# Turning the experts' middle rows with VectorE's 32x32 blocks and GpSimd moves instead of TensorE transposes

## What is computed

```
def _swiglu(x, w_gate, w_up, w_down):
    return (jax.nn.silu(x @ w_gate) * (x @ w_up)) @ w_down

def _moe(x, router, w_gate, w_up, w_down):
    xf = x.reshape(B * T, D)                       # 320 x 1024
    logits = (xf @ router).astype(jnp.float32)
    top_v, top_i = lax.top_k(logits, TOP_K)        # 2 of 8
    gates = jax.nn.softmax(top_v, axis=-1)
    combine = jnp.sum(jax.nn.one_hot(top_i, N_EXPERTS) * gates[..., None], axis=1)
    for e in range(N_EXPERTS):
        y = y + combine[:, e:e + 1] * _swiglu(xf, w_gate[e], w_up[e], w_down[e])
```

## Time and profile before

| | us |
|---|---|
| median of 3 runs | 1573.74 (1573.68 to 1573.88) |
| the profiled execution | 1574.41 |
| its span | 1572.9 |
| PE busy | 1554.9 (99%) |
| VectorE busy | 1296.5 (82%) |
| ScalarE busy | 1029.6 (65%) |
| GpSimd busy | 57.0 (4%) |
| mean granted clock of TensorE | 0.997 of full |

### The profile page before, as it was taken

The page is one execution under the profiler, slowest core; times in us unless marked ns, Lnnn a source line. Parts: engine busy times, 40 slices in busy tenths (PEclk is TensorE's granted clock), DMA queues, the critical chain, the costliest instruction groups (busy, mean ns, idle before and its releaser), DMA issues.

```text
span 1572.9 us, 23445 instructions
## 1 busy us (share of the span) xinstructions
PE 1554.9 (99%) x8467; PEld 1374.8 (87%) x8467; DVE 1296.5 (82%) x1534; ACT 1029.6 (65%) x1192; POOL 57.0 (4%) x89
## 2 busy tenths in 40 slices
PE   9999999999999999999999999999999999999997
PEld 8999999999989998888788888888888888888886
DVE  5578876766675678999899988989998999998996
ACT  4455433333354557788678878778778778777785
POOL 1002000000020010000200000000000001000000
PEclk9999999999999999999999999999999999999999
DMA  9625944444534344999999999999999999999992
GB/s 280 196 81 203 364 136 160 135 158 134 160 108 134 108 141 176 375 368 387 391 396 394 389 372 380 396 392 368 383 370 370 395 397 383 380 395 394 386 395 104
DMA packets 229906, 457.49 MB, mean 291 GB/s; under 512 B 10930, under 2 KB 73088, under 8 KB 229760
## 3 DMA queue, kind: packets, MB, share of 16 engines
q1 hardware_dynamic: 224288, 434.16, 76.3%
q0 software_dynamic: 5520, 22.04, 3.6%
HBM read 441.74 MB, written 17.58 MB: 292 GB/s over the span
## 4 chain that ended last, share of the span: by engine, by line
PE 91%; DVE 5%; DMA 2%; ACT 1%; issue 1%; SPq 0%; DVEq 0%; ACTq 0%
PE ps L1083 18%; PE ps L1058 12%; PE ps L1060 12%; PE ps L1059 12%; PE ps L681 11%; PE ps L683 10%; PE ps L682 10%; DVE wlo L1540 2%; PE ps L1096 1%; DMA raw<-in_moe_w_up 1%; DVE wlo L1535 1%; DMA proj<-in_x_prompt 0%; PE ps L1132 0%; ACT whi L1182 0%; PE ps L859 0%
## 5 line engine op out<-in xcount | busy, mean ns | idle before, releaser
L1540 DVE TENSOR_TENSOR wlo<-raw,whi 128x1024 fp32r<-128x1024 f32 x672 | 779.5, 1220 | 48.8 <-ACT whi L1186 47.5
L1186 ACT ACTIVATE whi<-raw 128x1024 fp32r<-128x1024 f32 x672 | 675.0, 1054 | 69.8 <-PE ps L1083 40.5
L1058 PE MATMUL ps<-whi,xg 128*128 128x512 f32 x896 | 354.7, 396 | 1.9 <-DVE wlo L1540 1.9
L1060 PE MATMUL ps<-whi,xg 128*128 128x512 f32 x896 | 350.1, 391 | 0.0
L1059 PE MATMUL ps<-wlo,xg 128*128 128x512 f32 x896 | 349.6, 390 | 0.0
L681 PE MATMUL ps<-xh,whi 128*128 128x322 f32 (+1 forms) x832 | 260.4, 313 | 1.6 <-DVE x L1928 1.1
L683 PE MATMUL ps<-xh,wlo 128*128 128x322 f32 (+1 forms) x832 | 257.6, 310 | 0.0
L682 PE MATMUL ps<-xl,whi 128*128 128x322 f32 (+1 forms) x832 | 257.6, 310 | 0.0
L1535 DVE TENSOR_TENSOR wlo<-raw,whi 128x2048 fp32r<-128x2048 f32 x72 | 165.0, 2293 | 55.3 <-ACT whi L1182 55.1
L1060 PEld LDWEIGHTS ps<-whi,xg 128*128 128x128 f32 x896 | 168.6, 188 | 36.0
L1058 PEld LDWEIGHTS ps<-whi,xg 128*128 128x128 f32 x896 | 168.6, 188 | 35.7 <-DVE wlo L1540 2.3
(11 more groups left out here) (368 smaller groups left out, 1470.9 us busy)
## 6 DMA issues: line engine op xcount, KB each, us to landing
raw<-in_moe_w_gate SPq DMA_DIRECT2D x112, 1024.0 KB, 8.7
raw<-in_moe_w_up SPq DMA_DIRECT2D x112, 1024.0 KB, 9.2
raw<-in_moe_w_down SPq DMA_DIRECT2D x112, 1024.0 KB, 8.7
raw<-in_w_in SPq DMA_DIRECT2D x23, 1024.0 KB, 6.1
raw<-in_ffn_w_gate SPq DMA_DIRECT2D x14, 1024.0 KB, 5.0
raw<-in_ffn_w_up SPq DMA_DIRECT2D x14, 1024.0 KB, 5.1
raw<-in_ffn_w_down SPq DMA_DIRECT2D x14, 1024.0 KB, 5.0
raw<-in_w_out SPq DMA_DIRECT2D x8, 1024.0 KB, 5.0
```

The costliest lines, as they stand in the source:

```text
L1058: pe.matmul(bank[:], xh_k, wh, start=k == 0, stop=False)
L1060: mm = pe.matmul(bank[:], xl_k, wh, start=False, stop=k == KT - 1)
L1186: act.activation(part(whi, n, SPLIT, h), part(raw, n, RAW, h), ACT.Copy).then_inc(hi_ready, 1)
L1540: dve.tensor_tensor(part(wlo, n, SPLIT, h), part(raw, n, RAW, h), part(whi, n, SPLIT, h).bitcast(F32), ALU.subtract).then_inc(lo_ready, 1)
```

## The change

In pairs 1 to 3, for chunks 1 to 12 of 14 (TURNED), TensorE no longer turns hm. Step "Z" (after down 0 of chunk c): VectorE transposes hm in 32x32 blocks within SBUF into hz, each block staying in its place of 32 partitions. GpSimd waits for it and copies 16 pieces of 32 partitions x 4 x 32 numbers to the partitions where they belong, into hT, also in SBUF. Step "R" (after gate 1 of the next chunk): ScalarE rounds hT into hT_hi, and VectorE makes hT_lo = hT - hT_hi. TensorE waits for hT_lo_ready before "down". Pair 0 keeps the old order (FIRST), and so do chunks 0 and 13 of each pair. hz and hT lie in u_mem, which earlier stages use.

On GpSimd, the copies of chunk c stand in line with the parks; the load of the next pair's rows comes after chunk 8's copies instead of right after the first park, and in the last pair GpSimd waits for its fetches to land before it goes on copying. To make room for three new semaphores, kd_turned, v_turned, kd_read and v_read are no longer kept per layer.

```diff
-    def pair_steps(last):
+    TURNED = range(1, PC - 1)
+
+    def pair_steps(first=False, last=False):
         steps = []
         for c in range(PC):
             steps.append(("gate", c, 0))
-            if c:
+            if c == 1 or c and first:
                 steps.append(("T", c - 1, 0))
             steps.append(("gate", c, 1))
+            if c > 1 and not first:
+                steps.append(("R", c - 1, 0))
...
             elif c:
-                steps += [("down", c - 1, 0), ("down", c - 1, 1)]
+                steps.append(("down", c - 1, 0))
+                if not first:
+                    steps.append(("Z", c, 0))
+                steps.append(("down", c - 1, 1))
...
+        hz = u_mem[:, 0:4 * P]
+        hT = u_mem[:, 4 * P:8 * P].rearrange("p (f s) -> p f s", f=4)
...
+            def turn_blocks(c, i):
+                pool.wait_ge(hz_ready, upto(c, i, PER_TURNS))
+                pool.wait_ge(hT_lo_ready, upto(c - 1, i, PER_TURNS))
+                pool.nop(nofuse=True)
+                z = hz.rearrange("p (f j s) -> p f j s", f=4, j=4)
+                for j in range(4):
+                    for q in range(4):
+                        ins = pool.tensor_copy(hT[32 * j:32 * j + 32, :, 32 * q:32 * q + 32], z[32 * q:32 * q + 32, :, j, :])
+                ins.then_inc(hT_copied, 1)
+
+            def pair(i):
+                for c in TURNED:
+                    turn_blocks(c, i)
+                    if c == 7:
+                        park(i, 0, y_parked)
+                    if c == 8:
+                        load_rows(i + 1 if isinstance(i, int) else pool.snap(i + 1))
                 park(i, 1, y_parked)
                 pool.wait_ge(y_parked, upto(48, i, 32))
...
             pool.wait_ge(rows_known, 1)
             fetch(0, y_1)
-            park(pairs, 0, last_parked)
-            pool.wait_ge(last_parked, 16)
-            fetch(1, y_2)
             for t in range(TT):
-                pool.wait_ge(y_fetched[1][t], 16)
+                pool.wait_ge(y_fetched[0][t], 16)
+            for c in TURNED:
+                turn_blocks(c, pairs)
+                if c == 7:
+                    park(pairs, 0, last_parked)
+                    pool.wait_ge(hT_copied, upto(c, pairs, PER_TURNS))
+                    pool.nop(nofuse=True)
+                    pool.wait_ge(last_parked, 16)
+                    fetch(1, y_2)
+                    for t in range(TT):
+                        pool.wait_ge(y_fetched[1][t], 16)
...
+                    if part == "R":          # ScalarE
+                        act.wait_ge(hT_copied, upto(c, i, PER_TURNS))
+                        act.activation(hT_hi[:, c % 2, :, :], hT, ACT.Copy).then_inc(hT_hi_ready, 1)
+                        continue
...
+                    if part == "Z":          # VectorE
+                        dve.wait_ge(m_hid, upto(c + 2, i, PC))
+                        dve.wait_ge(hT_copied, upto(c - 1, i, PER_TURNS))
+                        dve.transpose(hz, hm[:, c % 2, :]).then_inc(hz_ready, 1)
+                        continue
+                    if part == "R":
+                        turns += 1
+                        dve.wait_ge(hT_hi_ready, upto(turns, i, PC))
+                        dve.tensor_tensor(hT_lo[:, c % 2, :, :], hT, hT_hi[:, c % 2, :, :].bitcast(F32), ALU.subtract
+                                          ).then_inc(hT_lo_ready, 1)
+                        continue
...
-                            pe.wait_ge(job_read, upto(turned[c], i, PER_JOBS))
+                            if first or c not in TURNED:
+                                pe.wait_ge(job_read, upto(turned[c], i, per_jobs))
+                            else:
+                                pe.wait_ge(hT_lo_ready, upto(c, i, PER_TURNS))
```

More of the change, by code:

```diff
@@ L112, in pair_steps, with units_of, jobs_of @@
             elif c:
-                steps += [("down", c - 1, 0), ("down", c - 1, 1)]
+                steps.append(("down", c - 1, 0))
+                if not first:
+                    steps.append(("Z", c, 0))
+                steps.append(("down", c - 1, 1))
         return steps + [("down", PC - 1, 0), ("down", PC - 1, 1)]
-    PAIR, FINAL = pair_steps(False), pair_steps(True)
-    UNITS = [s for s in PAIR if s[0] in ("gate", "up", "down")]
-    assert UNITS == [s for s in FINAL if s[0] in ("gate", "up", "down")]
+    def units_of(steps):
+        return [s for s in steps if s[0] in ("gate", "up", "down")]
+    def jobs_of(steps):
+        return sum(s[0] in ("T", "X", "GT") for s in steps)
+    FIRST, PAIR, FINAL = pair_steps(first=True), pair_steps(), pair_steps(last=True)
+    UNITS = units_of(PAIR)
+    assert UNITS == units_of(FINAL) == units_of(FIRST)
     PER_PAIR = len(UNITS)
-    PER_JOBS = len(PAIR) - PER_PAIR
-    LAST_JOBS = len(FINAL) - PER_PAIR
-    assert PER_PAIR % RAW == 0 and PER_PAIR % SPLIT == 0 and PER_JOBS % 2 == 0
+    PER_JOBS = jobs_of(PAIR)
+    PER_TURNS = len(TURNED)
+    assert PER_PAIR % RAW == 0 and PER_PAIR % SPLIT == 0 and PER_JOBS % 2 == 0 and jobs_of(FIRST) % 2 == 0
     ctx = ExitStack()
@@ L339, in hybrid_stream_step @@
         proj_ready, gate_act, gate_dve = (by_layer(n) for n in ("proj_ready", "gate_act", "gate_dve"))
-        kd_turned, v_turned, kd_read, v_read, score_done, score_read = (by_layer(n) for n in (
-            "kd_turned", "v_turned", "kd_read", "v_read", "score_done", "score_read"))
+        kd_turned, v_turned, kd_read, v_read = (sem(n) for n in ("kd_turned", "v_turned", "kd_read", "v_read"))
+        score_done, score_read = (by_layer(n) for n in ("score_done", "score_read"))
         ds_done, st_step, o_done, o_sq, ms_act, og_step = (by_layer(n) for n in (
@@ L802, in turn_kv @@
                                               ident[:])
-                        mm.then_inc(v_turned[l], 1)
+                        mm.then_inc(v_turned, 1)
                 def scores():
-                    pe.wait_ge(v_read[l], 1)
+                    pe.wait_ge(v_read, 3 * l + 1)
                     for h in range(VT):
                         mm = pe.transpose(ps[6][0:DEC, P * h:P * h + P], proj[:, TV + h, 2 * P:T], ident[:])
-                    mm.then_inc(v_turned[l], 1)
-                    pe.wait_ge(kd_read[l], 2)
+                    mm.then_inc(v_turned, 1)
+                    pe.wait_ge(kd_read, 2 * l + 2)
                     for n, (t, pair) in enumerate((t, pair) for t in range(2) for pair in range(PAIRS)):
@@ L842, in states @@
                                 mm.then_inc(score_done[l], 1)
-                    pe.wait_ge(v_read[l], 3)
+                    pe.wait_ge(v_read, 3 * l + 3)
                     for t in range(LAST // 2):
@@ L1038, in pair @@
             def pair(i, steps, first=False):
-                unit, job = 0, GATHERS
+                unit, job, per_jobs = 0, *((GATHERS, jobs_of(FIRST)) if first else (FIRST_JOB, PER_JOBS))
                 for part, c, half in steps:
                     a, fc = c // FC, c % FC
+                    if part in ("Z", "R"):
+                        continue
                     if first and (part, c, half) == ("gate", 1, 0):
@@ L1163, in _ @@
             router()
-            pair(0, PAIR, first=True)
+            pair(0, FIRST, first=True)
             pe.wait_ge(ctl_ready, 1)
@@ L1692, in read_kd @@
                 def read_kd():
[L1693 to L1696, removed]
+                    dve.wait_ge(kd_turned, 2 * l + 1)
+                    dve.tensor_copy(kd_tok[:, 0:512], ps[4][:]).then_inc(kd_read, 1)
+                    dve.wait_ge(kd_turned, 2 * l + 2)
+                    dve.tensor_copy(kd_tok[0:DEC, 512:768], ps[5][0:DEC, 0:256]).then_inc(kd_read, 1)
                 def mask_scores():
@@ L2262, in _ @@
             step = router()
-            pair(0, PAIR, step, first=True)
+            pair(0, FIRST, step, first=True)
             dve.wait_ge(ctl_ready, 1)
```

37 lines of the change are left out of this document (22 added, 15 removed).

## The result

| | before | after |
|---|---|---|
| median, us | 1573.71 (4 runs) | 1719.08 (4 runs, 1718.05 to 1720.22) |
| ratio | | 1.0925, 95% interval 1.0911 to 1.0938 |
| span of the profiled execution | 1572.9 | 1718.3 |
| PE, VectorE, ScalarE, GpSimd busy | 99, 82, 65, 4% | 93, 77, 60, 24% |

The changed kernel is 145.4 us slower. The prediction was 1725, with 1590 to 1805 as range.

What follows compares the result with a forecast made beforehand. PE (TensorE), fed without a gap, was taken to bound the kernel before, VectorE's period after. Sum: 1574.4 + 144 (36 chunks) - 6 (stock) + 4 + 9 (last pair) = 1725.4, 1725 against the median; range 1590 to 1805.

Steps and rivals of the forecast that it cites:

- TensorE's saving, 0.47 us a chunk: On PE, four transposes leave each of 36 chunks, 0.47 us a chunk, 16.9 us on the path.
- Block transpose, 0.60 us: VectorE's added 128x512 transpose in step Z was taken to cost 0.60 us a chunk, like hm.
- Price of a copy, 0.30 us: One undisturbed GpSimd copy of 32 partitions x 128 elements was taken at 0.30 us, between 0.10 and 0.53.
- Copies done in the window, 4 of 16: Between Z and hT_lo, four copies get in at six boundaries of VectorE's subtractions; the other 12 run while VectorE waits.
- Toll, 0.10 us a copy: Each copy pushed in between subtractions delays VectorE's next instruction about 0.10 us, 0.4 us a chunk for four.
- The stand: VectorE stands ahead of hT_lo for 12 x 0.30 = 3.6 us of copies and 0.65 us for ScalarE's hT_hi.
- Chunk, 20.8 us: VectorE's period sets the chunk: 15.74 + 0.4 + 3.6 + 0.65 + 0.4 = 20.8 us against 16.8, 144 us over 36.
- Last pair, 4 + 9 us: Last pair: 4 us once for chunk 8's copies after the fetches, 9 us for VectorE's eight extra instructions.
- Swallowed by the stock, -6: In each of three pairs, PE's units in stock swallow the first 2 us of delay, -6 us.
- The clock costs nothing: A half clock after PE's gaps of 3 to 5 us a chunk fits into its idle time and costs nothing.
- (a): Rival: copies slip in, hT_hi is ready in time, PE stays the bound, 1559 us; chance 0.15.
- (b): Rival: all 16 copies end in the window but each holds VectorE 0.1 us, 1594 us; chance 0.10.

Runs made afterwards that it cites:

- one copy: Changed kernel with only the last of each chunk's 16 GpSimd copies left in, the other 15 blocks of hT keeping old values: 1564.97 us, ratio 0.9944 to the kernel before.
- the runs with 4, 8 and 16 copies: Changed kernel with four or eight of each chunk's 16 GpSimd copies left in: 1572.5 and 1627.7 us; 16 is the changed kernel itself, 1719.08 us.
- the run with memsets: Changed kernel with each chunk's 16 GpSimd copies replaced by 24 memsets, 16 into hT and 8 into a free part of u_mem: 1568.3 us.
- the run with TensorE kept busy: Changed kernel with 13 idle matmuls into a free bank in TensorE's gap before "down" of chunks 1 to 11: 1717.75 us, ratio 1.0912.
- every third chunk: Changed kernel turning only chunks 2, 5, 8, 11 of pairs 1 and 2 the new way, with ten subtractions in the window; other pairs as before: 1590.87 us.
- one copy and the last pair as before: Changed kernel with one of 16 copies left in for pairs 1 and 2, last pair turning and fetching as before the change: 1562.99 us, ratio 0.9932.

## Why the prediction was right

*TensorE's saving, 0.47 us a chunk.* Right: 16.32 instead of 16.80 us with one copy, 11.5 us over 24 chunks.

*Block transpose, 0.60 us.* It takes 0.63 us to the next row, and no more than 710 ns:

```profile
L2215 DVE STREAM_TRANSPOSE u_mem<-hm x36: 702/706/710, 869.1 to 1672.1; 128x512 f32<-128x512 f32 x36
```

*Price of a copy, 0.30 us.* 0.33 alone.

*Copies done in the window, 4 of 16.* Wrong for 33 of the 36 chunks: six, one at each boundary, the sixth as VectorE stops (in three of them a few more slip into a short pause of VectorE). I had read the 3.62 us row as a boundary lost, and weighed the Trainium skill's rule (SBUF — State Buffer, "Who interferes with whom": whoever comes first has the pair) down by it. The chunks of pairs 1 and 2, and the runs with 4, 8 and 16 copies there, agree with the strict queue. But boundaries are lost as well, as in the earlier trace rows: four in a row in chunks 5 and 11 of the last pair, with two copies done. What makes a waiting read miss them stays open. The same section of the Trainium skill says that a GpSimd instruction which only writes does not contend with such a VectorE instruction; the run with memsets agrees, with 0.20 us for each.

*Toll, 0.10 us a copy.* 0.08 (1.30 against 1.22 us), five times a chunk: 0.4. The predicted 0.4 was four times 0.10.

*The stand.* Predicted 12 x 0.30 = 3.6 us of copies and 0.65 for hT_hi; measured 3.5 (ten copies and the tail of the sixth) and 0.67 of the 4.17 us ahead of hT_lo. Too many copies left over (12) at too low a price (0.30) made nearly the right sum, which is luck: by the same working, six in the window and 0.33 each give 15.74 + 0.4 + 3.3 + 0.65 + 0.4 = 20.5.

*Chunk, 20.8 us.* 20.5, so 36 x 3.7 = 133 us instead of 144.

*Last pair, 4 + 9 us.* From the starts of its copies, chunk 8 came 3.4 us late and the chunks with combine and its like 10.5 us in sum: 13.9 against 13. Some 2 of the 10.5 us are not VectorE's extra work but the copies that missed boundaries in chunks 5 and 11 (VectorE's extra standing less the toll saved); they stand in for part of the predicted 9. In pair 1, ScalarE's three scalings of acc, which I had not counted, took 0.6 us each.

*Swallowed by the stock, -6.* Too much. 133.2 + 13.9 + 1.7 = 148.8 against 145.4 measured leaves -3.4. The first hm of pairs 1, 2 and 3 starts at 854.9, 1137.9 and 1418.2 us, before the change at 856.3, 1093.5 and 1330.6. So 1.4 us of the 3.4 were gained ahead of pair 1, where the first hm starts at 854.2 to 856.5 us in all these runs, and about 2 us are left for all three pairs together, where I had 2 for each.

*The sum.* 1725 against 1719 is closer than its terms: the chunk was 11 us too dear over 36 chunks, and against that the stock took 4 us less than I gave it, the scalings and the last pair cost 2.6 us more, and the stretch ahead of pair 1 differs by 1.4 (the other way).

*The clock costs nothing.* Right, by the run with TensorE kept busy. Where TensorE sets the pace, as with every third chunk, it does cost.

*Rivals.* That the copies end in time, as (a) and (b) have it, holds for four of them, which cost nothing in pairs 1 and 2, and no longer for eight. The 1559 us given for (a) was too low even so: the last pair gives back its own 5.6 us and 2 to 3 more. The lowest median of these runs is 1563, with one copy and the last pair as before.

No version here beats the kernel before and computes the same.

## What to carry to other kernels

Before moving work to GpSimd, count instructions and boundaries, not microseconds: next to a VectorE that streams instructions with two inputs in SBUF, GpSimd gets at best one SBUF-reading instruction done for each of VectorE's, however short its own is (0.23 and 0.29 us here). A second engine that works for 15.1 of 16.8 us, as VectorE did before the change, is then no spare room: its idle time must hold what is left over, and the consumer must come later than that. If a wait of an operand is moved, ask which of the units in stock need that very operand.

## What the runs showed of the hardware

- A GpSimd copy of 32 x 128 float32 takes 0.33 us start to start alone, 0.27 with half the elements, 1.23 beside 1.22 us subtractions; the subtraction behind it grows by 0.08 us, far less than the copy's 0.29.
- A GpSimd memset of the same 32 x 128 takes 0.20 us beside the same subtractions and delays none.
- In two chunks of the last pair, in every version that has copies beside subtractions there, a copy misses three or more boundaries between VectorE's subtractions in a row (5.64 us in the changed kernel). Both chunks come behind a combine on 64 partitions; the cause is open.
- After gaps of 2 to 5 us in the changed kernel TensorE was granted 1.2 GHz at the start of the next work; with the gaps filled the mean clock was 0.994 instead of 0.960, and the time the same.
